# Another order for the first loads of a decoder block: x and weights ahead of the constants, and the first splits moved

## The chip, the cores and the metric

One Trainium2 chip, one of its cores. The metric is the device time of one execution in microseconds. The kernel before took 1349.44 us (median of three runs, 1345.58 to 1349.54).

## The reference

One layer of a hybrid decoder trunk over 256 tokens of width 2048 with 16 meta tokens ahead of them, all in fp32:

```python
h = concat([pad, meta, x])
u = rmsnorm(h, norm_attn_pre)
qa, ka, va, qb, kb, vb, ga, gb = split(u @ w_in)
ya = diff_attention(qa, ka, va, rel_bias[:, :8], lam, diff_norm)     # 8 heads, causal
yb = swa_sink_attention(qb, kb, vb, rel_bias[:, 8:], sinks)          # 16 heads, window 128, meta keys
mix = sigmoid(ga) * (ya @ w_branch_a) + sigmoid(gb) * (yb @ w_branch_b)
h = h + rmsnorm(mix @ w_out, norm_attn_post)
h = h + rmsnorm(square(relu(rmsnorm(h, norm_ff_pre) @ w_ff1)) @ w_ff2, norm_ff_post)
```

## The kernel before

Each fp32 product is made of three products of split numbers: every operand is kept as a high half in fp32r and a low half (what the high half leaves over), and TensorE adds high x high, high x low and low x high. So each weight passes two engines before TensorE may use it: ScalarE copies raw into w_hi (split_hi, L418), VectorE writes raw minus w_hi into w_lo (split_lo, L781).

The weights stream in chunks of columns, and a chunk in eight units (UNITS) of its 2048 rows. raw, w_hi and w_lo have eight slots; SP loads a slot again once TensorE has used it (semaphore used). The engines run programs written out by hand, each with its own order, and meet in semaphores. Chunk 0 is the keys and values of the windowed attention (256 columns, loads of 256 KB, L317); from chunk 1 on a load has 512 KB (L338).

The head, which the change touches, does this:

- SP (L319 to L330) issues ident (the identity that transposes need), g_rows (the gain of the first norm), the first quarter of x (512 of its 2048 columns, into xs), relx and buck (the bias table's operands), then weights 0 and 1, and so on by twos: the next quarter of x ahead of weights 2, 4 and 6. ACT's queue issues the meta tokens xm alone (L432).
- TensorE makes five products on zeros (stay_busy, L1310), turns g_rows (L1315), the meta tokens (turn_meta, L1374) and x (turn_x(i), L1285: four 128x128 transposes for the unit i of 256 columns), makes the two products of the bias table (bias_table, L1392), and then chunk 0. Its first unit is parted: the four high x high products (multiply_high, L1321) need only the high halves; then come, for each unit, L1332 to L1334. Between the units of chunk 0 it turns x two to four units ahead, and waits there for the quarter of x.
- ScalarE squares the meta tokens (L453), copies the scaled meta tokens to their high half (L456), and then for each unit takes x out of PSUM, times the gain, into u_hi (keep_x, L441, two instructions), splits the weights (split_hi, L418), and after each second unit squares a quarter of x (square_x, L449). After unit 7 it goes on with the splits of chunk 1.
- VectorE copies the gain out of PSUM (L800), scales the meta tokens (L807), writes their low half (L822), and then for each unit the low half of x (keep_x, L815, two instructions) and of the weights (split_lo), after each second unit the other half of the squares (L830). After unit 7 come a sum (L833) and the low halves of chunk 1.
- GpSimd loads small parameters once weights 7 have landed, and stores the bias table to memory and reads it back skewed, much later.

ScalarE and VectorE work strictly in their order. TensorE's first product of chunk 1 (L1345) needs the low half of chunk 1's first weights.

## Time and profile before

| | |
|---|---|
| median of 3 runs | 1349.44 us (1345.58, 1349.44, 1349.54) |
| the profiled execution | 1345.25 us, its span on the core 1343.4 us |
| TensorE busy | 1332.1 us, 99% of the span |
| VectorE busy | 795.4 us, 59% |
| ScalarE busy | 623.9 us, 46% |
| GpSimd busy | 47.2 us, 4% |
| granted TensorE clock, mean | 0.998 |
| DMA | 252.58 MB, mean 188 GB/s |

The profile is of one execution, by the hardware profiler. Lines such as L1345 are lines of the kernel. PE is TensorE's products, PEld its loads of the stationary operand, DVE is VectorE, ACT ScalarE, POOL GpSimd, SP SyncE; a q behind a name (SPq) marks the issuing of transfers. Products overlap: one's duration is longer than the step to the next. Times of a timeline count from the span's start.

### The profile page before, as it was taken

The numbers are of one execution on the slowest core, as the hardware profiler recorded it, in microseconds if no ns is written. First come the engines' busy times: TensorE is split into PE (matmuls) and PEld (weight loads), VectorE is DVE, ScalarE is ACT, GpSimd is POOL, SyncE is SP. The second block draws the span as 40 slices with busy tenths as digits, with TensorE's granted clock in tenths as the row PEclk, the third lists the DMA queues.
The fourth block names the chain that finished last, engine by engine and source line by source line (L and its number), as shares of the span: only waits on it lengthen the run. The fifth ranks groups of instructions, "written<-read, shape, count | busy, mean of one in ns | idle before, by whom it ended". The sixth has DMA issues, their size and how long they took to land.

```text
span 1343.4 us, 19219 instructions
## 1 busy us (share of the span) xinstructions
PE 1332.1 (99%) x7157; PEld 1139.5 (85%) x7157; DVE 795.4 (59%) x1092; ACT 623.9 (46%) x901; POOL 47.2 (4%) x87
## 2 busy tenths in 40 slices
PE   9999999999999999999999999999999999999997
PEld 8889989888888888888988888888888888888886
DVE  7665564677765555547766545565546565456554
ACT  7454444455664434444644334443344444344442
POOL 1222110000000000000010000000000000000000
PEclk9999999999999999999999999999999999999999
DMA  9765555555466665774766666666666666666663
GB/s 285 211 183 164 166 166 150 159 162 155 142 189 189 189 197 197 239 236 158 247 190 190 190 196 192 189 189 190 196 185 190 191 194 191 193 190 191 191 190 107
DMA packets 146713, 252.58 MB, mean 188 GB/s; under 512 B 8483, under 2 KB 43727, under 8 KB 146236
## 3 DMA queue, kind: packets, MB, share of 16 engines
q1 hardware_dynamic: 142924, 241.39, 58.6%
q0 software_dynamic: 2160, 4.74, 1.8%
q10 hardware_dynamic: 1552, 5.37, 1.1%
q8 instruction: 55, 0.90, 0.3%
q14 instruction: 22, 0.18, 0.0%
HBM read 249.29 MB, written 2.17 MB: 187 GB/s over the span
## 4 chain that ended last, share of the span: by engine, by line
PE 98%; DVE 1%; DMA 1%; SPq 0%; issue 0%; ACT 0%; DVEq 0%; ACTq 0%
PE bank L1297 17%; PE bank L1299 17%; PE bank L1298 17%; PE bank L1626 16%; PE bank L1629 9%; PE bank L1345 4%; PE bank L1332 3%; PE bank L1334 3%; PE bank L1333 3%; PE bank L1347 2%; PE bank L1650 1%; PE bank L1285 1%; DMA xs<-in_x 1%; PE bank L1653 1%; PE bank L1436 1%; PE bank L1435 1%
## 5 line engine op out<-in xcount | busy, mean ns | idle before, releaser
L781 DVE TENSOR_TENSOR w_lo<-raw,w_hi 128x1024 fp32r<-128x1024 f32 (+1 forms) x456 | 549.8, 1214 | 433.0 <-ACT w_hi L418 431.8
L418 ACT ACTIVATE w_hi<-raw 128x1024 fp32r<-128x1024 f32 (+1 forms) x456 | 474.2, 1050 | 486.4 <-DMA raw<-in_w_ff 360.1
L1626 PE MATMUL bank<-f_hl,w_hi 128*128 128x512 f32 x960 | 229.8, 391 | 0.5 <-issue 0.5
L1626 PEld LDWEIGHTS bank<-f_hl,w_hi 128*128 128x128 f32 x960 | 176.4, 188 | 34.9 <-issue 0.9
L1298 PE MATMUL bank<-w_lo,hid_hi 128*128 128x512 f32 x512 | 199.3, 389 | 0.0
L1299 PE MATMUL bank<-w_hi,hid_lo 128*128 128x512 f32 x512 | 199.3, 389 | 0.0
L1297 PE MATMUL bank<-w_hi,hid_hi 128*128 128x512 f32 x512 | 199.3, 389 | 0.0
L1629 PEld LDWEIGHTS bank<-f_hl,w_lo 128*128 128x128 f32 x960 | 123.1, 191 | 4.7
L1629 PE MATMUL bank<-f_hl,w_lo 128*128 128x256 f32 x960 | 124.6, 283 | 0.0
L1298 PEld LDWEIGHTS bank<-w_lo,hid_hi 128*128 128x128 f32 x512 | 96.2, 188 | 19.9
L1297 PEld LDWEIGHTS bank<-w_hi,hid_hi 128*128 128x128 f32 x512 | 96.1, 188 | 19.9
L1299 PEld LDWEIGHTS bank<-w_hi,hid_lo 128*128 128x128 f32 x512 | 96.2, 188 | 19.9
L1297 PE MATMUL bank<-w_hi,u_hl 128*128 128x512 f32 x256 | 102.8, 402 | 0.0
L1299 PE MATMUL bank<-w_hi,u_hl 128*128 128x512 f32 x256 | 100.0, 391 | 0.0
L1298 PE MATMUL bank<-w_lo,u_hl 128*128 128x512 f32 x256 | 99.8, 390 | 0.0
L1332 PE MATMUL bank<-u_hl,w_hi 128*128 128x272 f32 x284 | 83.4, 294 | 0.0
L1333 PE MATMUL bank<-u_hl,w_lo 128*128 128x272 f32 x288 | 83.0, 289 | 0.2 <-DVE w_lo L781 0.2
L1334 PE MATMUL bank<-u_hl,w_hi 128*128 128x272 f32 x288 | 83.0, 288 | 0.0
L504 ACT ACTIVATE t<-t,sc 128x145 f32<-128x145 f32 (+1 forms) x64 | 29.3, 459 | 86.1 <-DVE sc L961 86.1
L1345 PE MATMUL bank<-u_hl,w_hi 128*128 128x512 f32 x256 | 62.8, 394 | 0.0
L1297 PEld LDWEIGHTS bank<-w_hi,u_hl 128*128 128x128 f32 x256 | 48.1, 188 | 12.3 <-issue 2.5
L1299 PEld LDWEIGHTS bank<-w_hi,u_hl 128*128 128x128 f32 x256 | 48.1, 188 | 10.4
(236 smaller groups left out, 1502.3 us busy)
## 6 DMA issues: line engine op xcount, KB each, us to landing
raw<-in_w_ff SPq DMA_DIRECT2D x256, 512.0 KB, 3.7
raw<-in_w_in SPq DMA_DIRECT2D x128, 512.0 KB, 3.7
raw<-in_w_out SPq DMA_DIRECT2D x32, 512.0 KB, 4.4
raw<-in_w_branch_b SPq DMA_DIRECT2D x16, 512.0 KB, 3.8
raw<-in_w_branch_a SPq DMA_DIRECT2D x16, 512.0 KB, 3.7
xs<-in_x SPq DMA_DIRECT2D x4, 512.0 KB, 7.3
raw<-in_w_in SPq DMA_DIRECT2D x8, 256.0 KB, 7.6
bias<-bias_table POOLq DMA_DIRECT2D x8, 256.0 KB, 4.6
```

The source lines that it names most:

```text
L418: act.activation(w_hi[:, u, :, 0:width], raw[:, u, :, 0:width], ACT.Copy).then_inc(hi_ready, 1)
L504: last = act.activation(t[:, e, a:b], t[:, e, a:b], ACT.Exp, bias=nmx[:, 2 * e + q:2 * e + q + 1], accum_out=sums[:, 2 * e + q:2 * e + q + 1])
L781: dve.tensor_tensor(w_lo[:, u, :, 0:width], raw[:, u, :, 0:width], w_hi[:, u, :, 0:width].bitcast(F32), ALU.subtract).then_inc(lo_ready, 1)
L1297: pe.matmul(ps[b][:, 0:width], hi_of(kt, b), wh, start=a, stop=False)
L1298: pe.matmul(ps[b][:, 0:width], hi_of(kt, b), wl, start=False, stop=False)
L1299: ins = pe.matmul(ps[b][:, 0:width], lo_of(kt, b), wh, start=False, stop=z)
L1332: pe.matmul(out, wh[:, k, cols], u_hi[:, kt, 0:KEYS], start=a, stop=False)
L1333: pe.matmul(out, wl[:, k, cols], u_hi[:, kt, 0:KEYS], start=False, stop=False)
L1334: ins = pe.matmul(out, wh[:, k, cols], u_lo[:, kt, 0:KEYS], start=False, stop=z)
L1345: ins = pe.matmul(out, wh[:, k, cols], u_hl[:, :, kt, 0:SEQ], start=kt == 0, stop=kt == KT - 1)
L1626: ins = pe.matmul(acc[g][:], w_hi[:, u, k, cols], f_hl[:, kt, :], start=kt == 0, stop=kt == KT - 1)
L1629: ins = pe.matmul(acc[g][:, 0:SEQ], w_lo[:, u, k, cols], f_hl[:, kt, 0:SEQ], start=False, stop=False)
```

## The change

It alters the order in the first 25 us; nothing else is touched.

- SP starts with the first half of x's first quarter (256 columns, semaphore x_first), weights 0, the second half, weights 1, and goes on as before. ident, g_rows, relx and buck leave SP's queue.
- ACT's queue issues ident, g_rows, xm, relx and buck, in this order, the last two behind a wait for relx's memset.
- ScalarE splits weights 0 ahead of x's unit 0, and squares the meta tokens after the first square of x. VectorE now makes the copy of the meta tokens' high half, and the low half of weights 0 ahead of the low half of x's unit 0.
- TensorE warms up with four products instead of five, turns unit 0 of x behind x_first, and makes the bias table's first product ahead of multiply_high and its second behind it.

```diff
@@ -220,6 +220,7 @@
         S0, S1, TB, MB = bank[4:8]
 
 
+        x_first = sem("x_first")
         x_landed = [sem(f"x_landed{i}") for i in range(4)]
         xm_landed, consts_landed, zeros_set = sem("xm_landed"), sem("consts_landed"), sem("zeros_set")
         rel_ones, rel_landed, small_landed = sem("rel_ones"), sem("rel_landed"), sem("small_landed")
@@ -316,17 +317,13 @@
                     sp.sem_inc(slot_free, 1)
                 sp.dma_start(raw[:, u, :, 0:width], unit_of(w, krange, nrange)).then_inc(landed[u], 16)
 
-            sp.dma_start(ident[:], identity).then_inc(consts_landed, 16)
-            sp.dma_start(g_rows[:], norm_attn_pre[0].rearrange("(k p) -> k p", p=P)).then_inc(consts_landed, 16)
-
             for u in range(UNITS):
-                if u % 2 == 0:
+                if u < 2:
+                    cols = slice(u * SEQ, (u + 1) * SEQ)
+                    sp.dma_start(xs[:, :, cols], xf[:, :, cols]).then_inc((x_first, x_landed[0])[u], 16)
+                elif u % 2 == 0:
                     cols = slice(u // 2 * CW, (u // 2 + 1) * CW)
                     sp.dma_start(xs[:, :, cols], xf[:, :, cols]).then_inc(x_landed[u // 2], 16)
-                if u == 0:
-                    sp.wait_ge(rel_ones, 1)
-                    sp.dma_start(relx[0:N_BUCKETS, :], rel_bias).then_inc(rel_landed, 16)
-                    sp.dma_start(buck[:], buckets).then_inc(rel_landed, 16)
                 load(u, w_in, slice(u * 256, u * 256 + 256), slice(KB0, KB0 + 256), None, 256)
             for c in range(1, C_MIX):
                 n0 = w_in_column(c)
@@ -429,7 +426,12 @@
                 else:
                     act.activation(dst, src, ACT.Identity, scale=scale).then_inc(turned_hi, 1)
 
+            act.dma_start(ident[:], identity).then_inc(consts_landed, 16)
+            act.dma_start(g_rows[:], norm_attn_pre[0].rearrange("(k p) -> k p", p=P)).then_inc(consts_landed, 16)
             act.dma_start(xm[:], meta_tokens).then_inc(xm_landed, 16)
+            act.wait_ge(rel_ones, 1)
+            act.dma_start(relx[0:N_BUCKETS, :], rel_bias).then_inc(rel_landed, 16)
+            act.dma_start(buck[:], buckets).then_inc(rel_landed, 16)
             act.wait_ge(eps_set, 1)
             act.activation(sc[:, 1:2], eps, ACT.Copy)
 
@@ -449,16 +451,17 @@
                 act.activation(gate_b[:, 0, :], xs[:, 0, j * CW:(j + 1) * CW], ACT.Square,
                                accum_out=ss3[:, j:j + 1]).then_inc(stats, 1)
 
-            act.wait_ge(xm_landed, 16)
-            act.activation(qaT[0:META].rearrange("p h t -> p (h t)"), xm[:], ACT.Square, accum_out=ssm[0:META, :]).then_inc(stats, 1)
+            split_hi(0, 0, 256)
             act.wait_ge(gain_ready, 1)
-            act.wait_ge(meta_scaled, 1)
-            act.activation(u_hi[:, :, SEQ:KEYS], meta_g[:], ACT.Copy).then_inc(meta_hi_ready, 1)
             for u in range(UNITS):
                 keep_x(u)
-                split_hi(u, 0, 256)
+                if u:
+                    split_hi(u, 0, 256)
                 if u % 2:
                     square_x(u // 2)
+                if u == 1:
+                    act.wait_ge(xm_landed, 16)
+                    act.activation(qaT[0:META].rearrange("p h t -> p (h t)"), xm[:], ACT.Square, accum_out=ssm[0:META, :]).then_inc(stats, 1)
 
             for u in range(UNITS - LEAD, UNITS):
                 split_ahead(0, u)
@@ -818,13 +821,17 @@
                 last.then_inc(turned_lo, 1)
 
             scale_meta()
+            dve.wait_ge(meta_scaled, 1)
+            dve.tensor_copy(u_hi[:, :, SEQ:KEYS], meta_g[:]).then_inc(meta_hi_ready, 1)
             dve.wait_ge(meta_hi_ready, 1)
             dve.tensor_tensor(u_lo[:, :, SEQ:KEYS], meta_g[:], u_hi[:, :, SEQ:KEYS].bitcast(F32), ALU.subtract)\
                .then_inc(meta_lo_ready, 1)
 
+            split_lo(0, 1, 256)
             for u in range(UNITS):
                 keep_x(u)
-                split_lo(u, u + 1, 256)
+                if u:
+                    split_lo(u, u + 1, 256)
                 if u % 2:
                     cols = slice(u // 2 * CW, (u // 2 + 1) * CW)
                     link(dve.tensor_tensor_reduce(rows[:, 1, :], xs[:, 1, cols], xs[:, 1, cols], 1.0, 0.0, ALU.mult,
@@ -834,7 +841,7 @@
                .then_inc(norm, 1)
             for u in range(UNITS - LEAD, UNITS - LEAD + 3):
                 split_ahead(0, u)
-            dve.wait_ge(table_ready, 1)
+            dve.wait_ge(table_ready, 2)
             for w in range(2):
                 last = dve.tensor_copy(rows[0:HA + HB, w, 0:TAB], bank[6 + w][0:HA + HB, 0:TAB])
             last.then_inc(table_copied, 1)
@@ -1310,7 +1317,7 @@
                     pe.matmul(bank[0][:, 0:256], rows[:, 0, 0:P], rows[:, 0, 0:256], start=True, stop=True)
 
             pe.wait_ge(zeros_set, 1)
-            stay_busy(5)
+            stay_busy(4)
             pe.wait_ge(consts_landed, 32)
             pe.transpose(bank[7][:, 0:KT], g_rows[:], ident[0:KT, 0:KT]).then_inc(gain_turned, 1)
 
@@ -1377,21 +1384,19 @@
 
             def turn_x(i):
 
-                pe.wait_ge(x_landed[i // 2], 16)
+                pe.wait_ge(x_landed[i // 2] if i else x_first, 16)
                 if i >= 4:
                     pe.wait_ge(turned_lo, i - 3)
                 turn4(bank[2 + i % 4], [xs[:, b, (2 * i + k) * P:(2 * i + k + 1) * P]
                                         for k in range(2) for b in range(BLOCKS)]).then_inc(turned, 1)
 
-            def bias_table():
+            def bias_table(w):
 
                 pe.wait_ge(rel_landed, 32)
                 pe.wait_ge(gain_ready, 1)
                 pe.wait_ge(meta_scaled, 1)
-                for w in range(2):
-                    ins = pe.matmul(bank[6 + w][0:HA + HB, 0:TAB], relx[:], buck[:, w, :], start=True,
-                                    stop=True)
-                ins.then_inc(table_ready, 1)
+                pe.matmul(bank[6 + w][0:HA + HB, 0:TAB], relx[:], buck[:, w, :], start=True,
+                          stop=True).then_inc(table_ready, 1)
 
             def turn_rows(kind, i):
                 n = TURN_NO[(kind, i)]
@@ -1517,11 +1522,12 @@
             turn_meta()
             turn_x(0)
             turn_x(1)
-            bias_table()
+            bias_table(0)
             pe.wait_ge(meta_hi_ready, 1)
             pe.wait_ge(turned_hi, 1)
             pe.wait_ge(hi_ready, 1)
             multiply_high(w_hi[:, 0], range(UK), acc_of(0))
+            bias_table(1)
             pe.wait_ge(meta_lo_ready, 1)
             for u in range(UNITS):
                 pe.wait_ge(turned_lo, u + 1)
```

## Rows read from the trace of the kernel before

**Rows 1.** The page's chain that ended last, by engine.

```profile
PE 98%; DVE 1%; DMA 1%; SPq 0%; issue 0%; ACT 0%; DVEq 0%; ACTq 0%
```

**Rows 2.** Waits of PE, whole span: line, releaser, us in total, times, longest.

```profile
PE bank L1285 <- DMA xs<-in_x: 0.8, 2, 0.5
```

**Rows 3.** Timeline of SP: start us, us, engine line op.

```profile
0.75 0.40 SPq L319 DMA_DIRECT2D ident<-in_identity  x1
...
1.68 0.41 SPq L325 DMA_DIRECT2D xs<-in_x  x1
2.13 1.08 SPq L328 DMA_DIRECT2D relx<-in_rel_bias  x1
...
3.73 0.91 SPq L317 DMA_DIRECT2D raw<-in_w_in  x2
```

**Rows 4.** DMA issues at 0.76 and 4.17: KB, us to landing.

```profile
xm<-in_meta_tokens ACTq DMA_DIRECT2D x1, 128.0 KB, 3.7
...
raw<-in_w_in SPq DMA_DIRECT2D x1, 256.0 KB, 5.3
```

**Rows 5.** Chain in order of time, 0 to 22: start us, us, what.

```profile
6.21 8.05 DMA xs<-in_x
```

**Rows 6.** Stretches: busy time by engine, PEclk, DMA share, GB/s.

```profile
2.00:4.00 2.00, 2.00 (x6) 1.53 (x6) 0.00 (x0) 0.69 (x2) 0.00 (x0) 1.00 0.69 141
...
12.00:14.00 2.00, 1.79 (x15) 1.57 (x13) 1.19 (x3) 2.00 (x6) 0.00 (x0) 1.00 1.06 384
```

**Rows 7.** Timeline of PE, 1 to 26.

```profile
1.20 3.90 PE L1310 MATMUL bank<-rows 128*128 128x256 f32 x10 [1.20 <-DVE rows L796]
...
4.50 0.59 PE L1310 MATMUL bank<-rows 128*128 128x256 f32 x2
5.11 1.14 PE L1374 MATMUL bank<-ident,xm 16*128 16x16 f32 x16
...
7.26 1.52 PE L1392 MATMUL bank<-buck,relx 33*24 33x400 f32 x4
...
9.68 0.36 PE L1333 MATMUL bank<-u_hl,w_lo 128*128 128x272 f32 x1 [0.20 <-DVE w_lo L781]
...
14.30 0.66 PE L1285 MATMUL bank<-ident,xs 128*128 128x128 f32 x4 [0.51 <-DMA xs<-in_x]
...
25.16 2.11 PE L1345 MATMUL bank<-u_hl,w_hi 128*128 128x512 f32 x8
```

**Rows 8.** Timeline of ACT, 1 to 15.

```profile
1.21 1.28 ACT L434 ACT_TABLE_LOAD   x1 [1.21 <-PEq L1708]
...
4.45 1.91 ACT L453 ACTIVATE qaT<-xm 16x2048 f32<-16x2048 f32 x1 [1.75 <-DMA xm<-in_meta_tokens]
7.20 0.82 ACT L441 ACTIVATE u_hl<-bank,g_col 128x256 fp32r<-128x256 f32 x2
7.92 0.63 ACT L418 ACTIVATE w_hi<-raw 128x512 fp32r<-128x512 f32 x1
9.54 0.63 ACT L418 ACTIVATE w_hi<-raw 128x512 fp32r<-128x512 f32 x1 [0.26 <-DMA raw<-in_w_in]
11.87 0.84 ACT L441 ACTIVATE u_hl<-bank,g_col 128x256 fp32r<-128x256 f32 x2 [1.09 <-PE bank L1285]
14.35 0.64 ACT L449 ACTIVATE gate_b<-xs 128x512 f32<-128x512 f32 x1
```

**Rows 9.** Timeline of DVE, 6 to 26.

```profile
6.36 0.42 DVE L807 TENSOR_TENSOR meta_g<-bank,g_col 128x256 f32<-128x256 f32 x1 [0.89 <-PE bank L1374]
...
12.81 0.88 DVE L815 SCALAR_TENSOR_TENSOR u_hl<-bank,g_col,u_hl 128x256 fp32r<-128x256 f32 x2 [1.28 <-ACT u_hl L441]
...
21.69 0.88 DVE L815 SCALAR_TENSOR_TENSOR u_hl<-bank,g_col,u_hl 128x256 fp32r<-128x256 f32 x2 [0.29 <-ACT u_hl L441]
...
23.89 2.35 DVE L781 TENSOR_TENSOR w_lo<-raw,w_hi 128x1024 fp32r<-128x1024 f32 x2
```

**Rows 10.** Groups of the first 25.2 us: xcount | busy us, mean ns | idle.

```profile
L781 DVE TENSOR_TENSOR w_lo<-raw,w_hi 128x512 fp32r<-128x512 f32 x8 | 5.5, 681 | 0.0
```

## The prediction

> **What bounds the kernel now.** I read the page's chain first. Nearly all of it is TensorE [rows 1], so a change at the head can only move the moment from which TensorE never waits again. The totals of TensorE's waits say how much there is to win there: over the whole execution it waits for x for 0.8 us in two places [rows 2], and the other waits of more than 0.2 us are the start itself (1.2 us) and two of 0.5 us at later hand-overs. The kernel is TensorE-bound behind the head, so whatever the head gives or costs arrives at the end one for one, and no more than that.
>
> (x comes in quarters of 512 columns, and each quarter feeds two of the eight units of 256 columns, numbered 0 to 7.) The chain in order of time names the wait that ends last: the third quarter of x, issued by SP at 6.21, lands 8.05 us later [rows 5], and TensorE turns it at 14.30 after 0.51 us without work [rows 7]. Before that it waited 0.3 us for the second quarter (the 0.8 less this 0.51, at 11.2) and 0.20 us for the low half of the first weights at 9.68 [rows 7]. From 14.30 to the first chunk's end at 25.16 it runs through.
>
> The chain does not show what comes second, and here that decides. Read VectorE beside it [rows 9]: from its 128x256 pair for unit 2 at 12.81 it works without a gap over 0.2 us until 21.40, waits 0.29 us, starts unit 7 at 21.69 and goes on into the split of the next chunk's first weights, 23.89 + 1.22 = 25.11 (1.22 is half of the 2.35 us of two, plus their overlap). TensorE begins that chunk at 25.16. VectorE is thus 0.05 us behind being the bound, with 0.29 us of slack in nine. It starts at 12.81 because ScalarE's copy of unit 2 starts at 11.87 [rows 8]. So three clocks run side by side: x's landing, ScalarE to VectorE, and TensorE's own work.
>
> **The change, part by part.**
>
> SP's queue. Between L319 at 0.75 and x at 1.68 lie 0.93 us of constants; between L328 at 2.13 and the first weights at 3.73 another 1.60 us, of which relx alone took 1.08 [rows 3]. These 2.53 us go, one further x issue comes in (0.46 us by the step from 1.68 to 2.13), so the first weights are issued 2.5 us sooner (at 1.21) and everything behind them 2.1 us sooner. SP loads nothing else here, and its next wait, for the first slot, ends with TensorE's first unit, which hardly moves.
>
> How much sooner do they land? The DMA queues moved 141 GB/s at a share of 0.69 from 2 to 4 us, and 384 GB/s at a share of 1.06 from 12 to 14 us [rows 6]. The early share leaves room, the late one none. Up to the third quarter of x the queues carry the constants (0.31 MB), 1.57 MB of x and four units of weights (1.05 MB), 2.9 MB. What can be won is the early hole: if 2 to 4.5 us runs at 200 to 270 GB/s, some 0.25 to 0.45 MB more is across, and at 330 to 384 GB/s that is 0.7 to 1.3 us. I take 1.0: the third quarter lands near 13.2. Bounds: 0 (bandwidth all the way) and 2.1 (the issue alone decides). The Trainium skill (DMA: Bandwidth & Descriptors, Issuing engines are not separate DMA queues) says that transfers of different issuing engines run on the same 16 DMA engines and interleave, and that a second issuer only saves issue time; this speaks against the change, and a gain of 0 to 0.2 us would follow from it at the third quarter. The row from 12 to 14 us agrees with it, the row from 2 to 4 us does not bind.
>
> ACT's queue. It now issues ident, g_rows, xm, relx and buck. With SP's durations [rows 3] these end near 3.7 us; behind them wait the table load (1.28 us [rows 8]), a small activation and the first weight split, done near 5.9 us. Their cover is ScalarE's idleness up to 7.2 us [rows 8]; it has 1.3 us left. ident and g_rows leave at the old times. xm goes out third, at 1.68 instead of 0.76. With its 3.7 us to landing [rows 4] it is there at 5.4, where TensorE turned it at 5.11 [rows 7]: 0.3 us later. By the 5.3 us of weights 1, which went out behind more work [rows 4], it would be 1.9 us later, so 0.3 to 1.9; I take 0.3, the same transfer's own figure on the same queue. buck keeps its time, near 7.2.
>
> Warm-up. One of five products goes. The ten passes took 3.90 us, the last two 0.59 from 4.50 [rows 7]: the passes came every 0.41 us at first (1.2 GHz) and every 0.21 at the end (2.4 GHz). Dropping the last two saves 0.42 us that ends before g_rows lands near 5.0, so it is worth 0.
>
> TensorE then: meta turned from 5.4 to 6.5 (1.14 us, row at 5.11), unit 0 of x to 7.1, unit 1, now with its own landing (about 6.4, needed at 7.0). The bias products took 1.52 us together [rows 7]; one now stands behind the first four products and fills the time in which TensorE waits for the low weights. Its sum is unchanged.
>
> ScalarE. The meta square (1.91 us and its read, 2.0 in all) ran at 4.45 in idle time; now it stands behind the first square of x, in front of the copy of unit 2. The meta copy (0.4 us) leaves ScalarE, the first weight split (0.53 us) moves ahead. The copy of unit 0 can start 0.07 us after its transposes end, 7.2, as in the row before [rows 8]. From 7.20 with steps read from start to start (0.72 for a pair of copies, by 7.20 to 7.92; the single split 0.63 less 0.1 of overlap; the square 0.64): 7.20 + 0.72 + 0.72 + 0.53 + 0.65 + 2.0 = 11.8. That is where the copy of unit 2 can start; it started at 11.87 before. So the moved square eats the whole of what the earlier x would give there: gain 0.07, not 0.7. Condition: the second weights must have landed by 8.64; they took 5.3 us from 4.17 [rows 4] and ScalarE waited for them until 9.54 [rows 8]. Issued at 2.1 with 1.3 MB to go I put them at 8.1 (7.4 to 9.0).
>
> VectorE. It gains a copy of 256 columns, at 0.42 us as its neighbour at 6.36 [rows 9], bounds 0.25 and 0.45. With meta's 0.3: scale 6.65, copy 7.1, low half 7.5, first weight split (0.68 [rows 10]) 7.95, x pair 8.6 to 9.45. The first unit's low products start at 9.55, before 9.68: gain 0.1. VectorE then waits until ScalarE's copy, 12.73, and runs to the end without the 0.29 us gap, as unit 7 is turned early enough (TensorE's turn ends near 20.2, its copy 21.1, wanted at 21.3).
>
> The sum at 25.16. TensorE's own work: the products of unit 2 follow the transposes of 14.30 at once. With unit 0 done 0.1 us sooner and the waits for the second and third quarter gone (0.8 together) it gains some 0.9. VectorE: 0.08 + 0.29 = 0.37, next chunk's weights at 24.74. The smaller gain holds, and it needs the third quarter only by 13.8. So the head is worth 0.4 us. The profiled execution took 1345.25 us with a span of 1343.4; it becomes 1344.9 with a span of 1343.0. It is one at the lower of two levels: the three timed runs were 1345.58, 1349.44 and 1349.54, with the median on the upper one. The change touches nothing that I can tie to these 4 us, so the sum on the median is 1349.44 - 0.4 = 1349.0.
>
> **Rivals.**
> 1. Forecast, the gain is what VectorE's slack allows, 0.1 to 0.7 us: 1349.0. Chance 0.48.
> 2. Nothing moves. The transfers are bound by bandwidth as in the row from 12 to 14 us, or the second weights land at 9.0 instead of 8.1, which puts ScalarE's copy at 12.2 and uses the 0.37 us up: 1349.4 (within 0.1). Chance 0.25. The Trainium skill's sentence above would make this the likelier one.
> 3. Slower by ScalarE's queue. The meta square is a block of 2.0 us in front of the copy of unit 2. From the point where xm lands more than 0.37 us later than 5.4 (in the ring behind ident and g_rows and beside SP's traffic), VectorE's run to 25.1 ends later than now. At the far bound above (1.6 us beyond 5.4) it costs 1.2 us, half way there 0.4: 1349.8 to 1350.6, by the middle 1350.0. For it speaks VectorE's 0.05 us distance from the bound; against it xm's 3.7 us beside x in the old run. Chance 0.13.
> 4. The whole hole closes: ScalarE's copies start sooner because xm lands as fast as it did when first (5.0), and the gain reaches 0.8 to 1.1 us: 1348.5. Chance 0.09.
> 5. The clock. Warm-up is 0.4 us shorter and a pause of up to 0.9 us may stand between it and meta. If the rise to 2.4 GHz came later, everything from there runs at 0.41 instead of 0.21 per pass. Up to 7.6 us this costs 0.44 us on the first transposes (result near 0), up to 14 us some 2.5 us: 1352. In the old run the rise came during the eighth pass or so. Chance 0.05.
>
> **How the numbers follow.** A measurement of this kernel tells about 0.3% (4 us) from no change. All five cases lie inside that; only a median that falls on the other level crosses it, or nearly so. Against 1349.44, a median at 1345.2 is faster by 0.31%; I give 0.11 for that, 0.03 for slower, 0.86 for the same. The range must hold both levels less the gain and the cost of rival 3: from 1345.25 - 0.7 = 1344.5 to 1349.44 + 1.2 = 1350.6; it leaves out rival 5.
>
> **What would show it.** Right: SP's first weights issued near 1.2 and the third quarter of x near 4.1; ScalarE's meta square near 9.8, with unit 2's copy starting at its end near 11.8; VectorE without a gap from 12.7; the first 128x512 product of TensorE near 24.8; behind it nothing but a shift. Wrong: that product before 24.3 (the slack argument fails, or ScalarE's queue was shorter) or after 25.2 (rival 3, then unit 2's copy starts after 12.2); the third quarter landing near 14.2 (rival 2); passes of 0.4 us behind 5 us (rival 5). The forecast as a whole is wrong if the two spans differ by more than 1 us.

## The result, and the profile after

| | kernel before | changed kernel |
|---|---|---|
| median | 1346.41 us (20 runs, 1344.8 to 1349.74) | 1350.86 us (20 runs, 1350.31 to 1353.15) |
| profiled execution | 1345.25, span 1343.4 | 1352.78, span 1351.0 |

The ratio is 1.0031, 95% interval 1.0024 to 1.0039: the change makes the kernel slower, by 4.4 us. The forecast was 0.4 us faster. With more runs the kernel before shows its two levels: 13 of 20 runs from 1344.8 to 1346.65 and 7 from 1349.1 to 1349.7. The median of the first three had stood on the upper one. (The lower level has two parts, below and above some 1345.7; in the runs taken beside the experiments the granted clock of the whole run is 0.998 to 0.999 in the first part and mostly 0.997 in the second. No run of the second part was profiled.)

TensorE's largest waits in the changed kernel (line, releaser, us in total, times, longest us). The waits for x of [rows 2] are gone, and a larger one has come, for the meta tokens:

```profile
PE bank L1381 <- DMA xm<-in_meta_tokens: 1.7, 1, 1.7
PE bank L1317 <- DVE rows L799: 1.2, 1, 1.2
PE bank L1656 <- ACT w_hi L415: 0.7, 1, 0.7
PE bank L1632 <- issue: 0.5, 1, 0.5
PE bank L1292 <- DVE f_hl L794: 0.5, 1, 0.5
```

The transfers, as issue lines of the changed kernel, xm's issued at 1.76 and the third quarter's at 4.69 (KB, us to landing):

```profile
xm<-in_meta_tokens ACTq DMA_DIRECT2D x1, 128.0 KB, 5.1
...
xs<-in_x SPq DMA_DIRECT2D x1, 512.0 KB, 7.5
```

x's third quarter lands at 12.2 instead of 14.26 [rows 5], 2.1 us sooner: SP issues it 1.5 us sooner (4.69 against 6.21), and it takes 7.5 us instead of 8.05. The meta tokens land at 6.9 instead of 4.45. TensorE's head shows what that did in the profiled execution (timeline: start, us, engine, line, operation; L1317, L1381, L1398 and L1292 are L1310, L1374, L1392 and L1285 of before, L1340 and L1352 are L1333 and L1345):

```profile
1.20 3.78 PE L1317 MATMUL bank<-rows 128*128 128x256 f32 x8 [1.20 <-DVE rows L799]
...
6.92 1.88 PE L1381 MATMUL bank<-ident,xm 16*128 16x16 f32 x16 [1.72 <-DMA xm<-in_meta_tokens]
8.73 1.97 PE L1292 MATMUL bank<-ident,xs 128*128 128x128 f32 x8
10.63 1.53 PE L1398 MATMUL bank<-buck,relx 33*24 33x400 f32 x2
...
14.74 0.59 PE L1340 MATMUL bank<-u_hl,w_lo 128*128 128x272 f32 x1
...
20.25 0.43 PE L1341 MATMUL bank<-u_hl,w_hi 128*128 128x272 f32 x1
20.47 0.42 PE L1339 MATMUL bank<-u_hl,w_hi 128*128 128x272 f32 x1
20.70 0.32 PE L1340 MATMUL bank<-u_hl,w_lo 128*128 128x272 f32 x1
20.86 0.29 PE L1341 MATMUL bank<-u_hl,w_hi 128*128 128x272 f32 x1
...
31.81 1.43 PE L1352 MATMUL bank<-u_hl,w_hi 128*128 128x512 f32 x5
```

Two bias passes now take 1.53 us, where four took 1.52 [rows 7]. The eight transposes of x take 1.97 us, where before they took 1.09. From one product to the next pass 0.23 us until 20.7 and 0.12 to 0.13 after that. TensorE thus ran at 1.2 GHz until 20.7 us; in the execution of before it reached 2.4 GHz at 4.5. (The granted clock of these rows' stretches stands at 1.00 all the same, as it does for the slow warm-up passes in [rows 6]; here only the step between products tells the level.)

The first 128x512 product comes at 31.81 against 25.16 [rows 7], 6.65 us later. Of these, 1.81 are there when meta's turning starts (6.92 against 5.11). The rest, 4.8 us, builds up behind it, in the stretch with the low clock; a_busy8 below tests whether the clock is the reason. The two profiled executions differ by 7.5 us; the remaining 0.9 is mostly a single wait of 0.7 us for a high half of weights (L1656, near the middle), which the other executions of this study show at 0.2 us or not at all.

ScalarE in the changed kernel, the meta square and what follows it:

```profile
12.60 1.89 ACT L464 ACTIVATE qaT<-xm 16x2048 f32<-16x2048 f32 x1
14.40 0.18 ACT L464 ACTIVATION_READ_ACCUMULATOR qaT<-xm 16x1 f32 x1
...
17.82 0.84 ACT L443 ACTIVATE u_hl<-bank,g_col 128x256 fp32r<-128x256 f32 x2 [3.23 <-PE bank L1292]
```

The square ends 3.2 us before its follower can start. In this execution TensorE is so late that ScalarE's queue costs nothing.

The profiled execution is not the typical one. A clock that rises late leaves no mark in the granted clock, but one that falls does: in the profiled executions below it is 0.994 and 0.996 for the whole run where the clock rose and fell again (a_busy5, b_loads), and 0.998 where it only rose late (b_busy4_again, a_oldloads, a_xm_first, and this one). Of the changed kernel's 20 runs, 12 stand at 0.993 to 0.995 (ten of them 1350.3 to 1351.1 us, two 1353.1) and 8, with the profiled one, at 0.998 or 0.999 (1350.7 to 1352.8). So in most of its runs the clock will have risen and been lost again. That is worked out from these figures; no such run of the changed kernel itself was profiled.

### The profile page after: what moved, and what is told of

Same layout as the page of the kernel before. It is cut to its first block, busy times and chain, and to the rows that moved or that the text cites. A ratio compares the mean times of both kernels' runs of the same rounds, so it can differ in the third digit from the quotient of the medians.

```text
span 1351.0 us, 19217 instructions
## 1 busy us (share of the span) xinstructions
PE 1338.2 (99%) x7155; PEld 1143.6 (85%) x7155; DVE 795.5 (59%) x1093; ACT 624.0 (46%) x900; POOL 45.6 (3%) x87
## 4 chain that ended last, share of the span: by engine, by line
PE 98%; DMA 1%; DVE 1%; ACT 0%; issue 0%; ACTq 0%; DVEq 0%; SPq 0%
PE bank L1304 17%; PE bank L1306 17%; PE bank L1305 17%; PE bank L1632 16%; PE bank L1635 8%; PE bank L1352 4%; PE bank L1339 3%; PE bank L1340 3%; PE bank L1341 3%; PE bank L1354 2%; PE bank L1292 1%; PE bank L1656 1%; PE bank L1659 1%; PE bank L1441 1%; PE bank L1440 1%; DMA raw<-in_w_ff 0%
## 5 line engine op out<-in xcount | busy, mean ns | idle before, releaser
L1340 PE MATMUL bank<-u_hl,w_lo 128*128 128x272 f32 x288 | 84.2, 292 | 0.0
L1352 PE MATMUL bank<-u_hl,w_hi 128*128 128x512 f32 x256 | 62.8, 394 | 0.0
```

The costliest lines, as they stand in the source:

```text
L1340: pe.matmul(out, wl[:, k, cols], u_hi[:, kt, 0:KEYS], start=False, stop=False)
L1352: ins = pe.matmul(out, wh[:, k, cols], u_hl[:, :, kt, 0:SEQ], start=kt == 0, stop=kt == KT - 1)
```

## Experiments

A measure first. In the profiled execution of every kernel below but the changed one, the device time less the start of TensorE's first 128x512 product (the end of the head) is 1320.0 us, give or take 0.6; in the changed one it is 1321.0, with the wait of 0.7 us named above. So nearly all that these kernels gain or lose arises in the head, and that start tells the time. A difference of a few tenths between two single profiled times need not come from the head.

| kernel | meta turned from | first 128x512 | profiled time | median of its runs | lowest to highest |
|---|---|---|---|---|---|
| before | 5.11 | 25.16 | 1345.25 | 1346.4 | 1344.8 to 1349.7 |
| b_copy | 5.68 | 25.54 | 1345.52 | one run | |
| b_busy4 | 5.04 | 25.11 | 1345.67 | 1348.68 | 3 to 1345.9, 7 from 1348.6 |
| b_busy4_again | 5.04 | 28.91 | 1348.88 | one run | |
| b_busy7 | 6.34 | 25.82 | 1345.90 | 1346.21 | 1345.1 to 1348.1 |
| b_loads | 6.83 | 28.33 | 1348.25 | 1350.12 | 1348.3 to 1350.8 |
| a_oldloads | 5.04 | 29.10 | 1348.96 | 1348.98 | 1346.6 to 1350.0 |
| a_old_b7 | 6.95 | 26.23 | 1346.22 | 1346.75 | 1345.9 to 1347.4 |
| changed | 6.92 | 31.81 | 1352.78 | 1350.86 | 1350.3 to 1353.2 |
| a_busy5 | 7.70 | 31.00 | 1351.04 | 1350.63 | 1348.7 to 1351.8 |
| a_busy8 | 6.84 | 26.11 | 1346.19 | 1346.52 | 1346.1 to 1347.7 |
| a_fill | 7.69 | 26.98 | 1346.93 | 1347.15 | 1346.6 to 1349.2 |
| a_xm_first | 6.56 | 31.00 | 1350.58 | 1350.50 | 1348.3 to 1351.2 |
| c_consts_sp | 6.11 | 25.38 | 1345.42 | 1346.15 | 1345.4 to 1346.7 |
| d_early_sq7 | 7.19 | 26.28 | 1346.39 | 1346.18 | 1345.2 to 1347.1 |
| d_early_sq5 | 5.73 | 24.82 | 1344.78 | 1346.01 | 1344.8 to 1350.1 |
| d_early_sq6 | 5.98 | 25.07 | 1345.68 | 1345.70 | 1344.6 to 1346.4 |

**The warm-up product alone.** The kernel before, with

```diff
-            stay_busy(5)
+            stay_busy(4)
```

> The kernel before with four warm-up products instead of five, and nothing else. Theory A (the clock is the cause: with one product less TensorE's engine clock does not rise to 2.4 GHz before the first real work): the warm-up's eight passes stay at 0.43 us, transposes at about 0.22 us a piece, the first 128x512 product starts near 29 to 31 instead of 25.2 us, and the time is 2.5 to 5 us above the kernel before. Theory B (meta tokens' late landing and the square in ScalarE's queue are the cause, the warm-up is free): the first 128x512 product within 0.3 us of 25.2, time the same.

Measured: 1348.68 against 1346.32 us, ratio 1.0010 (0.9997 to 1.0022). By the medians' interval that is not clear of no change. But its ten runs fall on both sides: three near 1345.7 and seven near 1348.8, where the kernel before, run beside it, has 23 of 31 on its lower level. The first profile is of a run on the lower side. A second one, of the same kernel, met the upper side:

> The kernel before with four warm-up products, a second time. Three of its ten runs lay near 1345.7, seven near 1348.8. If the upper level is a clock that has not risen by the first real work, a profile that falls on it shows products at 0.43 us up to 14 us or later and the first 128x512 product near 28.5 to 29; one on the lower level shows it near 25.1 as the last one did.

The same lines of the two executions, first b_busy4:

```profile
1.20 3.78 PE L1310 MATMUL bank<-rows 128*128 128x256 f32 x8 [1.20 <-DVE rows L796]
...
5.04 1.41 PE L1374 MATMUL bank<-ident,xm 16*128 16x16 f32 x16
6.38 1.09 PE L1285 MATMUL bank<-ident,xs 128*128 128x128 f32 x8
...
25.11 2.11 PE L1345 MATMUL bank<-u_hl,w_hi 128*128 128x512 f32 x8
```

then b_busy4_again:

```profile
1.20 3.78 PE L1310 MATMUL bank<-rows 128*128 128x256 f32 x8 [1.20 <-DVE rows L796]
...
5.04 1.86 PE L1374 MATMUL bank<-ident,xm 16*128 16x16 f32 x16
6.83 1.97 PE L1285 MATMUL bank<-ident,xs 128*128 128x128 f32 x8
...
17.02 0.37 PE L1333 MATMUL bank<-u_hl,w_lo 128*128 128x272 f32 x1
17.23 0.29 PE L1334 MATMUL bank<-u_hl,w_hi 128*128 128x272 f32 x1
...
28.91 2.12 PE L1345 MATMUL bank<-u_hl,w_hi 128*128 128x512 f32 x8
```

One program, with the warm-up and the start of meta equal to 0.01 us. In the first the clock rises during meta's turning, in the second at 17.1 us; that is 3.8 us at the first 128x512 product and 3.2 us in the time. So this kernel's two levels are the clock in the head. The kernel before, profiled once more, with no edit:

> The kernel before, unchanged, a second profile. Its runs lie in three groups, 1344.4 to 1345.5, 1346.1 to 1346.9 and 1349.5. By the clock theory the time less the start of the first 128x512 product is 1320.1 (within 0.6) on whichever group it falls: 24.5 to 25.4, 26 to 26.8 or 29.4 us, and products at 0.43 us stand behind 5 us in the upper two.

It gave 1345.52 us with the product at 25.54, the ten warm-up passes taking 4.47 us instead of 3.90: the rise came later, but still inside the warm-up (meta's turning took 1.14 us, as at the high clock). Its upper level itself was not caught in a profile. That it is the same effect is argued from the four-product kernel and from the next run.

**A longer warm-up.** The kernel before with stay_busy(7):

> The kernel before with seven warm-up products instead of five, and nothing else. The runs of the kernel before lie on two levels, near 1345 to 1346.6 and near 1349.4 us. If the levels are runs in which the clock had risen by the fifth product and runs in which it had not: with seven the upper level is gone, all runs lie between 1345 and 1347, the median near 1345.7; the price of the two products (0.4 us at the high clock, up to 0.9 at the low) shows as a meta start near 5.5 to 6 instead of 5.1 us. If the levels have another cause: both stay, about a third of the runs near 1349.5.

Measured: 1346.21 us, ratio 0.9995 (0.9985 to 1.0005). The group at 1349.5 is gone; eight of ten runs lie under 1346.7, two at 1347.3 and 1348.1. The median is 0.5 us above what was expected, and so is meta's start (6.34 instead of 5.5 to 6): what the lost upper level gives, the later start costs. In the six kernels of this study that have six or more warm-up products ahead of g_rows, none of 64 runs lies above 1348.1, where the kernel before has a fifth to a third of its runs above 1349.

**The queues alone.** The kernel before, with SP's and ACT's queues of the change, five products, and the splits and the square where they were:

```diff
-            sp.dma_start(ident[:], identity).then_inc(consts_landed, 16)
-            sp.dma_start(g_rows[:], ...).then_inc(consts_landed, 16)
...
+                    sp.dma_start(xs[:, :, cols], xf[:, :, cols]).then_inc((x_first, x_landed[0])[u], 16)
...
+            act.dma_start(ident[:], identity).then_inc(consts_landed, 16)
+            act.dma_start(g_rows[:], ...).then_inc(consts_landed, 16)
             act.dma_start(xm[:], meta_tokens).then_inc(xm_landed, 16)
```

> The kernel before with only the queues changed as in the change (x and weights first on SP, constants on ACT's queue behind one another, first quarter of x halved); five warm-up products, the meta square and all splits where they were. If the loads alone are the cause: meta tokens land near 6.9 us instead of 4.45, x's third quarter near 12.2 instead of 14.3, TensorE waits 1.5 us for the meta tokens, and the clock may fall or not rise: first 128x512 product 27 to 32 us, time 2 to 5 us above. If the fifth product is what counts: the clock rises near 4.3 us as before, first 128x512 product near 25.5 to 26.5 us, time 0.3 to 1.3 us above the kernel before.

Measured: 1350.12 us, ratio 1.0024 (1.0013 to 1.0035). The first reading holds: five products don't save it. TensorE waited 0.79 us for the meta tokens and started them at 6.83. The clock was up by then: turning them took 1.16 us, as at 2.4 GHz, where the slow clock takes 1.86. It fell only afterwards (stretch: busy time of each engine, then PEclk, DMA share, GB/s):

```profile
7.00:9.00 2.00, 2.00 (x25) 1.81 (x25) 0.42 (x1) 2.00 (x3) 0.00 (x0) 1.00 1.02 325
9.00:11.00 2.00, 2.00 (x6) 0.44 (x6) 1.56 (x4) 2.00 (x7) 0.00 (x0) 0.72 1.08 398
...
15.00:17.00 2.00, 2.00 (x11) 2.00 (x11) 1.25 (x3) 2.00 (x6) 0.33 (x1) 0.57 0.93 284
17.00:19.00 2.00, 2.00 (x19) 2.00 (x18) 2.00 (x5) 1.88 (x6) 2.00 (x5) 1.00 0.53 59
```

By these shares it fell at 9.9 and was back at 16.7. Nine of its ten runs have a granted clock of 0.994 to 0.996, so they lost the clock in this way; the profiled one is the fastest of the ten.

**The rest of the change alone.** The changed kernel with the queues of before, so with four products:

```diff
-            act.dma_start(ident[:], identity).then_inc(consts_landed, 16)
-            act.dma_start(g_rows[:], ...).then_inc(consts_landed, 16)
...
+            sp.dma_start(ident[:], identity).then_inc(consts_landed, 16)
+            sp.dma_start(g_rows[:], ...).then_inc(consts_landed, 16)
```

> The changed kernel with the queues of before (constants ahead of x on SP, meta tokens alone on ACT's queue), so with four warm-up products, the parted bias products, the moved splits and the moved meta square. Clock theory: as with four products in the kernel before, some runs near 1345.3 and most near 1348.7, median 1348.5; in a run whose clock rises the first 128x512 product comes near 24.8 us. Loads theory (late meta tokens break the warm-up): they land at 4.45 us again, so it is 2 us or more below the changed kernel's 1350.9. If the moved meta square costs by itself: first 128x512 product above 25.5 us in a run whose clock rises.

Measured: 1348.98 us, ratio 1.0013 (1.0003 to 1.0023), seven of ten runs from 1348.9 to 1350.0. As expected by the clock, it is near the four-product kernel. So each half of the change by itself brings TensorE into a long low clock in most runs, in two ways: with the short warm-up the rise mostly comes late (in this profile near 17 us), with the new queues the clock is lost behind the pause. The two don't add up: 3.8 us for the queues alone, 2.7 for the rest alone, 4.4 together.

With seven products, the other half without the clock:

> The same with seven warm-up products, to take the clock out of it: what the moved splits, the parted bias products and the moved meta square are worth with the loads of before. Against the kernel before with seven products: 0.4 us less by the forecast of the head's sum (VectorE without its gap); 0 if third quarter of x, which lands at 14.3, decides; 0.3 to 0.6 us more if the meta square behind a later start (meta turned from 5.9 on) holds the copy of unit 2 up past 12.2.

Measured: 1346.75 us, ratio 0.9999 (0.9989 to 1.0010), against 1346.21 of b_busy7: no gain of 0.4, and in the profiles the product comes at 26.23 against 25.82. But meta had started 0.6 us later too (6.95 against 6.34), as the warm-up took longer in that execution. From meta's start it is 19.28 against 19.48 us, which does not show a gain either: the later start by itself took away the 0.4 us that b_busy7 waits for x. So what the moved splits are worth here stays open. The wait on low weights that they leave is the same as in c_consts_sp below.

**The changed kernel with TensorE kept busy.** stay_busy(8) instead of 4:

> The changed kernel with eight warm-up products instead of four, which fill TensorE's wait for the meta tokens (they landed at 6.9 us). Theory A: the clock rises before 5.5 us, the first 128x512 product comes near 25.5 to 27 us instead of 31.8, and the time is 4 to 6 us below the changed kernel, that is -1 to +1.5 us of the kernel before. Theory B: the meta tokens land as late as before, and the time stays within 1 us of the changed kernel's 1350.9.

Measured: 1346.52 us, 4.3 below the changed kernel, ratio to before 1.0002 (0.9992 to 1.0012), all ten runs between 1346.1 and 1347.7. The lines:

```profile
1.20 5.63 PE L1317 MATMUL bank<-rows 128*128 128x256 f32 x16 [1.20 <-DVE rows L799]
6.75 0.23 PE L1322 MATMUL bank<-ident,g_rows 16*128 16x16 f32 x1
6.84 1.14 PE L1381 MATMUL bank<-ident,xm 16*128 16x16 f32 x16
...
26.11 2.08 PE L1352 MATMUL bank<-u_hl,w_hi 128*128 128x512 f32 x8
```

Meta starts at 6.84, as late as in the changed kernel (6.92), and the 128x512 product comes 5.7 us sooner. This separates the two causes: with meta equally late, the clock is worth 4.3 us of median. The late meta tokens as such are worth 0.95 us in the profiles (26.11 against 25.16, and 1346.19 against 1345.25 us). Of that the medians show only 0.2, because the kernel before has its upper level in them and a_busy8 has none. The 0.95 us come by the way that rival 3 described: ScalarE's copy of unit 2 starts behind the meta square, at 13.14 instead of 11.87, and TensorE waits 0.40 us for low weights, until 15.67.

One product more, five instead of four:

> The changed kernel with five warm-up products instead of four. If the dropped product is the whole cause: it comes down to the kernel before, 1346 to 1347. If the late meta tokens break the warm-up by themselves (as in the kernel before with the new queues, 1350.1): it stays at 1349.5 to 1350.9, with TensorE's products at 0.43 us behind the wait.

Measured: 1350.63 us, ratio 1.0028 (1.0016 to 1.0039): no better. In this execution too the clock was up and fell, so that the rows show it (stretch, as for b_loads):

```profile
5.00:7.00 2.00, 0.71 (x3) 0.24 (x2) 0.17 (x1) 0.63 (x1) 0.00 (x0) 1.00 1.06 239
7.00:9.00 2.00, 1.30 (x17) 1.27 (x18) 0.00 (x0) 0.00 (x0) 0.00 (x0) 0.89 1.04 325
9.00:11.00 2.00, 2.00 (x9) 1.63 (x10) 1.75 (x5) 0.87 (x3) 0.00 (x0) 0.50 1.08 399
...
17.00:19.00 2.00, 2.00 (x12) 2.00 (x11) 0.07 (x1) 1.00 (x3) 2.00 (x4) 0.55 0.22 11
19.00:21.00 2.00, 2.00 (x18) 2.00 (x18) 2.00 (x5) 2.00 (x6) 1.07 (x3) 1.00 0.84 185
```

The warm-up ended at 5.6 with the clock up; then TensorE had almost nothing until 7.70 and turned the meta tokens until 8.9; near 8.6 the clock fell to 0.50 and came back near 18.8. Seven of its ten runs stand at 0.994 to 0.996. So the wait for the meta tokens costs the clock even where the warm-up had brought it up, and the dropped product, put back, changes next to nothing in this kernel (0.2 us).

The same eight products, four of them behind g_rows:

```diff
             pe.transpose(bank[7][:, 0:KT], g_rows[:], ident[0:KT, 0:KT]).then_inc(gain_turned, 1)
+            stay_busy(4)
```

> The changed kernel, four warm-up products where they are and four more between the turning of g_rows and the wait for the meta tokens: the same eight as in a_busy8, but the wait for the gain is not behind them. If what counts is that TensorE has work through the wait for the meta tokens, it does the same as a_busy8: one level, 1346.0 to 1346.7, first 128x512 product near 26. If the unbroken stretch ahead of g_rows counts: the clock still does not rise in part of the runs, and runs above 1348 appear.

Measured: 1347.15 us, seven runs from 1346.6 to 1347.2 and three at 1348.3 to 1349.2, ratio 1.0003 (0.9992 to 1.0015). Its profile has the meta tokens landing later still (meta from 7.69) and 0.41 us of wait left. It does most of what a_busy8 does, not all; why three runs lie higher was not taken apart.

**Which transfer stands third.** The changed kernel with the meta tokens first on ACT's queue:

```diff
+            act.dma_start(xm[:], meta_tokens).then_inc(xm_landed, 16)
             act.dma_start(ident[:], identity).then_inc(consts_landed, 16)
             act.dma_start(g_rows[:], ...).then_inc(consts_landed, 16)
-            act.dma_start(xm[:], meta_tokens).then_inc(xm_landed, 16)
```

> The changed kernel with the meta tokens issued first on ACT's queue, ahead of ident and g_rows. Landing theory (the wait of 1.7 us for the meta tokens costs its time and breaks the warm-up): they land near 4.5 us, TensorE turns them at about 5.5 us (g_rows now last, near 5.3), and the first 128x512 product comes near 25 to 26 us, time 0 to 1 us from the kernel before. Clock theory (four products alone are too few): meta starts at 5.5 us, 1.4 us sooner, but still at 1.2 GHz, first 128x512 product near 29 to 30.5 us, time 1.5 to 3 us below the changed kernel.

Measured: 1350.50 us, ratio 1.0027 (1.0017 to 1.0036). The 8 KB of g_rows, now third, took 4.6 us and landed at 6.4, where at second place they took 3.3. TensorE waits for them instead:

```profile
PE bank L1322 <- DMA g_rows<-in_norm_attn_pre: 1.5, 1, 1.5
```

Neither of my readings had this: I had g_rows near 5.3. In these two orders, beside SP's stream of x and weights, the third transfer of ACT's queue takes 4.6 us with 8 KB and 5.1 with 128.

**A better order.** ident and g_rows back to SP's head, xm first on ACT's queue, relx and buck behind it, x and weights of SP as in the change, seven products:

```diff
+            sp.dma_start(ident[:], identity).then_inc(consts_landed, 16)
+            sp.dma_start(g_rows[:], ...).then_inc(consts_landed, 16)
             for u in range(UNITS):
                 if u < 2:
...
-            stay_busy(4)
+            stay_busy(7)
```

> A candidate: the changed kernel with ident and g_rows back at the head of SP's queue, the meta tokens first on ACT's queue, relx and buck behind them, and seven warm-up products. Meta tokens land near 4.5 to 4.9, g_rows near 4.9, the third quarter of x near 13. By the clock theory all runs lie on one level; the first 128x512 product near 24.8 to 25.3, time 1344.6 to 1345.6, some 1 us below the median of the kernel before. If late constants return (SP's x beside them), g_rows lands after 5.5 but the clock still rises: 1345.5 to 1346.5.

Measured: 1346.15 us, ratio 0.9998 (0.9988 to 1.0007), all runs on one level, 1345.4 to 1346.7. The 1 us that was hoped for did not come: meta starts only at 6.11, when the seven products are done. It shows the effect of ScalarE's queue that the forecast had named. ScalarE first, then VectorE, then TensorE:

```profile
10.51 1.91 ACT L464 ACTIVATE qaT<-xm 16x2048 f32<-16x2048 f32 x1
12.32 0.18 ACT L464 ACTIVATION_READ_ACCUMULATOR qaT<-xm 16x1 f32 x1
12.41 0.81 ACT L443 ACTIVATE u_hl<-bank,g_col 128x256 fp32r<-128x256 f32 x2
...
13.32 0.88 DVE L818 SCALAR_TENSOR_TENSOR u_hl<-bank,g_col,u_hl 128x256 fp32r<-128x256 f32 x2 [1.36 <-ACT u_hl L443]
...
14.94 0.36 PE L1339 MATMUL bank<-u_hl,w_hi 128*128 128x272 f32 x1 [0.40 <-DVE w_lo L784]
```

The copy of unit 2 starts where the square's read ends, VectorE stands 1.36 us, and TensorE waits 0.40 us for unit 2's low weights, not for x. So the square was put back ahead of the first split:

```diff
+            act.wait_ge(xm_landed, 16)
+            act.activation(qaT[0:META]..., xm[:], ACT.Square, accum_out=ssm[0:META, :]).then_inc(stats, 1)
             split_hi(0, 0, 256)
```

> c_consts_sp with the meta square back at its old place, ahead of the first split, where ScalarE waits for weights anyway. ScalarE theory: the copy of unit 2 starts 0.4 us or more sooner than 12.41, when its transposes end, VectorE's gap of 1.36 us shrinks to about 1 us or less, TensorE's wait for the low weights (0.4 us) goes, the first 128x512 product comes near 25.0 instead of 25.38, median 1345.7 against 1346.15. If x's third quarter decides: TensorE waits for x there instead and nothing is gained.

Measured: 1346.18 us, ratio 0.9993 (0.9982 to 1.0004), no different from c_consts_sp. TensorE's wait for the low weights falls from 0.40 to 0.22 us, but in this execution the warm-up took 5.97 us instead of 4.89 and covers the rest. From meta's start to the 128x512 product it is 19.09 against 19.27 us, and again 19.09 in the two kernels below, whose meta starts at 5.73 and 5.98: the square's place is worth 0.2 us.

With five products:

> The same with five warm-up products. In runs whose clock rises in time, meta starts near 5.1 instead of 6.1 us and the first 128x512 product comes near 24.4: 1344.2 to 1344.8. If the rise is a matter of luck with five, as in the kernel before, a third or more of the runs lie 3 to 4 us higher, near 1348.5, and the median is no better than with seven.

Measured: 1346.01 us, ratio 0.9999 (0.9985 to 1.0013); six runs from 1344.8 to 1346.2 and four from 1347.8 to 1350.1. Its profile is the nearest to a plain measure of the new order of loads: beside b_copy, with as many warm-up products, meta starting within 0.05 us (5.73 against 5.68) and the clock up in both, the 128x512 product comes at 24.82 against 25.54 and the time is 1344.78 against 1345.52. With the clock kept, x and weights sooner, the moved splits and the parted bias products are thus worth some 0.7 us, in one execution of each. With six products:

> The candidate with six warm-up products, between five (lowest runs 1344.8, four of ten above 1347.7) and seven (1345.2 to 1347.1). If six still cover the rise: all runs from 1344.9 to 1346.8, median 1345.5, some 0.7 us under the kernel before. If not: one to three of twelve near 1348 to 1350, median 1346.

Measured: 1345.70 us, ratio 0.9989 (0.9979 to 0.9999), twelve runs between 1344.6 and 1346.4. This one is ahead of both kernels, of the kernel before by 0.7 us of median, just clear of noise, and of the changed one by 5.2. Most of the 0.7 is the upper level that is gone: against the lower level of the kernel before alone (median 1345.95 of those run beside it) it is 0.25 us.

## Why the prediction was wrong, point by point

**The bound.** Right: behind the head TensorE is saturated and a shift goes through one for one (the 1320.0 us above, 1321.0 in the changed kernel's profile).

**SP's queue.** Right in kind, short in size: the third quarter landed 2.1 us sooner, where 1.0 was taken. That it equals my upper bound is chance: the bound was 2.1 us of issue time, and SP issued it at 4.69 instead of the 4.1 that I had, 1.5 us sooner than before; the other 0.55 us is a shorter transfer. The early hole closed as supposed (259 GB/s from 2 to 4 us instead of 141 [rows 6]). The Trainium skill (DMA: Bandwidth & Descriptors, Issuing engines are not separate DMA queues) says that transfers of several issuing engines interleave on the same DMA engines and that only issue time is saved; the 0 to 0.2 us that I drew from it for this transfer is not what was measured. For the constants the trace agrees with it: from ACT's queue, beside SP's stream, xm took 5.1 us instead of 3.7. I had used that rule only on the transfer that the change wanted to speed up.

**xm.** The first step that failed. I took its old 3.7 us [rows 4] because it was the same transfer on the same queue. The bound beside it, the 5.3 us of weights 1, which had work ahead of it, was the right row: 5.1 was measured, and a_xm_first shows the same with g_rows. In these runs the landing time went with the place in the queue and the company, more than with the size of the transfer. And I had priced the delay only as a delay, in rival 3; that the pause in front of the meta tokens costs the clock was in no term of the sum.

**The clock, with the warm-up and with the pause.** The step that decided. The sum put the clock at nothing, in both terms that touch it. It priced the dropped product at 0, since it ended before g_rows landed; in the kernel before that product alone moves most runs 3 us up (b_busy4). And it priced the late meta tokens at their 0.3 us of delay; with the queues alone, and five products, the pause in front of them costs 3.8 us (b_loads). In the changed kernel the pause alone is enough: with the fifth product back it stays at 1350.63 (a_busy5), and most of its own runs show a clock that rose and fell. Work through the whole pause brings 4.3 us back (a_busy8). Rival 5 had the mechanism, a shorter warm-up and a pause of up to 0.9 us; the pause became 1.72 us, and the rival had a chance of 0.05 and a price of 2.5 us. The price is 3.2 us where the meta tokens are in time (b_busy4_again against b_busy4) and 4.3 with them late. I took the row of one execution, in which the rise came at 4.5 us, for a property of the kernel, though the three times stood in front of me on two levels 4 us apart: "The change touches nothing that I can tie to these 4 us" is the sentence that failed. It touched both things that they hang on, the length of the warm-up and what follows it.

**ScalarE's queue.** Right where the clock is up (c_consts_sp: copy at the end of the square, VectorE and not x the bound), and worth 0.2 us. In the changed kernel as measured it is hidden behind TensorE's slow head. That VectorE's 0.29 us gap would close and give 0.4 us was neither confirmed nor refuted. With the clock kept, the new order of loads gives 0.7 us (d_early_sq5 against b_copy), but that kernel has the constants on SP's queue, xm first and the square at its old place, so it does not measure the forecast's 0.4 us. Rival 3's block stands behind a_busy8's 0.95 us: it had 1.2 for xm 1.6 us beyond 5.4, and xm landed 1.5 beyond.

**The range.** 1350.6 ended 0.3 us under the median because the clock rival was left outside it. That it came so near is luck: the range stood on 1349.44, the upper level, while the kernel before has its median at 1346.41. For the same reason rival 3's 1350.6 looks almost right, and is not: its delay costs 0.95 us where the clock is kept.

## What to carry to other kernels

Filler products at the head buy the clock, not time: here it was kept in every run only where they lasted until the real work followed without a wait. Before dropping one, or before delaying what comes behind it, look at the spread of the runs. Levels some 3 us apart in a kernel whose profile begins with slow products suggest that the rise is already a matter of luck. The granted clock of each run then says which way it was lost: lower where it fell, unchanged where it only rose late. And a load moved to the other queue should be priced by a row of a transfer with as much ahead of it and beside it.

## What the runs showed of the hardware

- One program with one timeline up to 5.04 us got its clock during the following microsecond in one execution and at 17.1 us in another. The Trainium skill (TensorE: Matmul & The Clock Gate, Part 1) says that one kernel shows a different number of slow products from run to run; the trace agrees, with ten warm-up passes in 3.90 and in 4.47 us in two executions of the kernel before, and fourteen in 4.89 to 5.97 us in four kernels.
- A missed or lost rise costs 7 us or more of low clock, although TensorE is busy for most of it: 6.8 us in b_loads (9.9 to 16.7), 10.2 in a_busy5 (8.6 to 18.8), 12 behind the warm-up in b_busy4_again (5 to 17.1), and until 20.7 in the changed kernel. What in this head holds the rise back so long was not taken apart.
- A clock that was up fell behind a short pause: in a_busy5 after 1.98 us of waiting and 0.9 us of turning the meta tokens, in b_loads after 0.79 us of waiting and 3.1 us of work.
- The granted clock of the rows stands at 1.00 in stretches where the step between products is that of 1.2 GHz, if no fall came before (changed kernel to 20.7). Only where it fell do the rows show 0.50.
